# Four column blocks of a branch's output product as two pairs of seven half-size products, in a fused encoder layer

## The reference, cut to what matters

```python
y_a = o_a.reshape(B, S, GLA_HEADS * GLA_DV) @ w_gla_out      # branch A, 1024 x 1024 @ 1024 x 1024
...
y_b = o_b @ w_mla_out                                        # branch B, the same shape
g = jax.nn.sigmoid(gates.astype(jnp.float32)).astype(x.dtype)
merged = g[..., :D] * y_a + g[..., D:] * y_b
return merged @ w_o
```

## Time and profile before

| what | value |
| --- | --- |
| median of 3 runs | 1970.11 us (1969.41 to 1972.61) |
| the profiled execution: time | 1970.56 us |
| its span, first to last instruction | 1968.8 us |
| busy: PE, PEld, DVE, ACT, POOL | 1894.8, 1599.6, 1341.3, 1026.8, 136.4 us |
| mean granted TensorE clock | 0.987 |

### The profile page before, as it was taken

The page is one execution under the profiler, slowest core; times in us unless marked ns, Lnnn a source line. Parts: engine busy times, 40 slices in busy tenths (PEclk is TensorE's granted clock), DMA queues, the critical chain, the costliest instruction groups (busy, mean ns, idle before and its releaser), DMA issues.

```text
span 1968.8 us, 26535 instructions
## 1 busy us (share of the span) xinstructions
PE 1894.8 (96%) x9316; PEld 1599.6 (81%) x9316; DVE 1341.3 (68%) x1802; ACT 1026.8 (52%) x1681; POOL 136.4 (7%) x139
## 2 busy tenths in 40 slices
PE   7999999999999999999999999995699999999998
PEld 7988888888878888888888888885588888888886
DVE  4477777767864656556866334435799898898986
ACT  6465555555563424344534112222377777877775
POOL 1111110111000000000000000000010100101010
PEclk9999999999999999999999999998799999999999
DMA  6100000000311112021353542524899999999993
GB/s 206 43 24 11 23 17 23 17 23 12 118 55 44 55 33 65 21 73 61 124 175 133 173 127 88 191 110 175 314 364 401 394 398 399 389 400 389 398 395 81
DMA packets 146135, 322.04 MB, mean 164 GB/s; under 512 B 17920, under 2 KB 72576, under 8 KB 146048
## 3 DMA queue, kind: packets, MB, share of 16 engines
q1 hardware_dynamic: 141296, 304.09, 41.7%
q0 software_dynamic: 4752, 16.78, 3.4%
HBM read 283.07 MB, written 37.75 MB: 163 GB/s over the span
## 4 chain that ended last, share of the span: by engine, by line
PE 88%; DVE 8%; ACT 2%; issue 1%; DMA 1%; POOL 1%; SPq 0%; ACTq 0%; DVEq 0%; POOLq 0%
PE ps L968 23%; PE ps L970 23%; PE ps L969 23%; PE ps L957 7%; PE ps L1045 5%; PE ps L1254 1%; PE ps L1266 1%; PE ps L1085 1%; PE ps L1084 1%; DVE pT_lo L1521 1%; PE ps L1238 1%; PE ps L1398 1%; PE ps L1264 1%; DVE top_i L2203 1%; DVE qR L1702 1%
## 5 line engine op out<-in xcount | busy, mean ns | idle before, releaser
L1521 DVE TENSOR_TENSOR w_lo<-w_raw,w_hi 128x1024 fp32r<-128x1024 f32 x384 | 442.5, 1218 | 54.9 <-ACT w_hi L2721 54.7
L2721 ACT ACTIVATE w_hi<-w_raw 128x1024 fp32r<-128x1024 f32 x384 | 370.9, 1053 | 11.5 <-DMA w_raw<-in_w_gate_e 11.1
L968 PE MATMUL ps<-w_hi,xeT_hi 128*128 128x512 f32 x512 | 201.2, 393 | 1.8 <-DVE xeT_lo L1521 1.0
L970 PE MATMUL ps<-w_hi,xeT_lo 128*128 128x512 f32 x512 | 199.7, 390 | 0.0
L969 PE MATMUL ps<-w_lo,xeT_hi 128*128 128x512 f32 x512 | 199.2, 389 | 0.0
L1521 DVE TENSOR_TENSOR d_lo<-d_raw,d_hi 128x1024 fp32r<-128x1024 f32 (+1 forms) x64 | 68.1, 1072 | 168.0 <-ACT d_hi L2438 163.4
L1751 DVE TENSOR_REDUCE row_max<-ps 128x1 f32<-128x1024 f32 x64 | 78.3, 1223 | 104.5 <-PE ps L1085 104.4
L2438 ACT ACTIVATE d_hi<-d_raw 128x1024 fp32r<-128x1024 f32 x46 | 48.8, 1061 | 190.3 <-PE ps L970 130.5
L968 PE MATMUL ps<-hT_parts,d_hi 128*128 128x512 f32 x368 | 144.7, 393 | 0.8 <-DVE obS L1774 0.8
L970 PE MATMUL ps<-hT_parts,d_lo 128*128 128x512 f32 x368 | 143.4, 390 | 0.0
L969 PE MATMUL ps<-hT_parts,d_hi 128*128 128x512 f32 x368 | 143.3, 389 | 0.0
(11 more groups left out here) (368 smaller groups left out, 4209.8 us busy)
## 6 DMA issues: line engine op xcount, KB each, us to landing
w_raw<-in_w_gate_e SPq DMA_DIRECT2D x128, 512.0 KB, 7.2
w_raw<-in_w_up_e SPq DMA_DIRECT2D x128, 512.0 KB, 7.0
w_raw<-in_w_down_e SPq DMA_DIRECT2D x128, 512.0 KB, 5.9
d_raw<-in_w_in SPq DMA_DIRECT2D x80, 256.0 KB, 3.2
gates_T<-stage SPq DMA_DIRECT2D x16, 512.0 KB, 2.9
sg<-gates_T SPq DMA_DIRECT2D x16, 512.0 KB, 3.6
xs<-in_x SPq DMA_DIRECT2D x8, 512.0 KB, 12.9
rows_T<-hT SPq DMA_DIRECT2D x2, 2048.0 KB, 6.9
```

The costliest lines, as they stand in the source:

```text
L968: pe.matmul(out_ap, a_hi, b_hi, start=start, stop=False)
L970: return pe.matmul(out_ap, a_lo, b_hi, start=False, stop=stop)
L1521: return dve.tensor_tensor(dst, whole, high.bitcast(F32), ALU.subtract)
L2721: nc.scalar.activation(w_hi[:, n % RING, :], w_raw[:, n % RAW, :], ACT.Copy).then_inc(hi_ok, 1)
```

## The change

The last four blocks of branch B (jobs 12 to 15) become two pairs, numbered p = 6 and 7 behind the six gate pairs. They use the gate stage's scheme with roles changed: the operand is `oT` (branch B's rows), the weight blocks are i = 4, 5 and 6, 7 of `w_mla_out`. The operand sums, four sets of 4 sums with 3 low parts (and a fourth low part later), are made from raw rows that are loaded a second time, under jobs 8 to 11. Gating is done in halves (`y_gate`). Merged rows are all split behind the pairs, since the sums lie where their parts go. The changed lines, cut to those that carry the order:

```diff
@@ SyncE
+            def load_o(k):
+                if k == 0:
+                    sp.wait_ge(oT_lo_ok, 2 * KD)
+                elif k == 1:
+                    sp.wait_ge(d_used, Y0 + KD)
+                else:
+                    sp.wait_ge(o_lo_ok.sem, o_lo_ok.at(3 * (k - 1)))
+                for j in range(2):
+                    sp.dma_start((stage, o_raw_odd)[k % 2][:, j, :], ob_dram[KD // 2 * j + k]).then_inc(o_in[k].sem, 16)
...
-            for m in range(2 * KD):
-                if m + 2 < 2 * KD:
-                    load_job((m + 2) // KD, 1, (m + 2) % KD, Y0 + m + 2)
-                    load_gate(m + 2)
-                if 2 <= m + 2 < KD:
+            for m in range(Y_WHOLE - 2):
+                if m == KD:
+                    load_o(1)
+                load_job((m + 2) // KD, 1, (m + 2) % KD, Y0 + m + 2)
+                if m >= KD - 1 and m != KD + 1:
+                    load_o((0, 2)[m - KD + 1])
+                elif m == KD + 1:
+                    load_o(3)
+                load_gate(m + 2)
+                if m + 2 < KD:
                     load_stage(m + 2)
+            load_pair(PAIRS)
+            load_gate(KD + 4)
+            load_gate(KD + 5)
+            load_pair(PAIRS + 1)
+            load_gate(KD + 6)
+            load_gate(KD + 7)
@@ TensorE, in gate_products
+                    if p == PAIRS:
+                        pe.wait_ge(y_ev, KD + j // 2 + 1)
+                        if j in (2, 3):
+                            pe.wait_ge(o_lo_ok.sem, o_lo_ok.at(12 if j == 2 else 16))
...
-            for m in range(2 * KD):
+            for m in range(Y_WHOLE):
                 branch_job(m)
+            for p in range(PAIRS, PAIRS + Y_PAIRS):
+                gate_products(p)
@@ VectorE
+            def o_sums_of(k):
+                dve.wait_ge(o_in[k].sem, o_in[k].at(32))
+                b11, b12, b21, b22 = o_whole(0, k), o_whole(1, k), o_whole(2, k), o_last(k)
+                dve.tensor_tensor(b11, b12, b11, ALU.subtract).then_inc(o_sum.sem, 1)
+                dve.wait_ge(o_sum.sem, o_sum.at(4 * k + 1))
+                dve.tensor_tensor(b12, b22, b12, ALU.subtract).then_inc(o_sum.sem, 1)
+                dve.tensor_tensor(o_whole(3, k), b22, b11, ALU.subtract).then_inc(o_sum.sem, 1)
+                dve.wait_ge(o_sum.sem, o_sum.at(4 * k + 3))
+                dve.tensor_tensor(b21, b21, o_whole(3, k), ALU.subtract).then_inc(o_sum.sem, 1)
...
+            for k in range(4):
+                if k < 2:
+                    dense_lo(Y0 + KD + k + 2)
+                o_sums_of(k)
+                o_sums_low(k)
+                if k == 2:
+                    weight_sums(p, range(4))
+                elif k == 3:
+                    weights_low(p, (0, 1, 2, 3))
+                    for i in range(4):
+                        o_last_low(i)
+                    weights_low(p, (4,))
+                product(KD + k)
+            weights_low(p, (5, 6))
+            y_sum(p, 0)
+            y_gate(p, 0)
+            weight_sums(p + 1, range(4))
+            weights_low(p + 1, (0, 1))
```

More of the change, by code:

```diff
@@ L55 @@
 Y0 = MERGE0 + len(WHOLE)
-OUT0 = Y0 + 2 * KD
+Y_WHOLE = KD + 4
+Y_PAIRS = 2
+OUT0 = Y0 + Y_WHOLE
 CREDIT = 1
@@ L1347, in _ @@
                 gate_products(p)
-            for m in range(2 * KD):
+            for m in range(Y_WHOLE):
                 branch_job(m)
-            pe.wait_ge(y_ev, 2 * KD - 2)
-            halves_first = [(half, j) for half in range(2) for j in range(4)]
+            for p in range(PAIRS, PAIRS + Y_PAIRS):
+                gate_products(p)
+            free_first = {(0, 0): 1, (0, 2): 2, (0, 3): 4, (1, 2): 4, (1, 3): 4, (1, 1): 5, (0, 1): 6, (1, 0): 7}
             tiles_first = [(half, j) for j in range(4) for half in range(2)]
@@ L1364, in _ @@
                 pe.wait_ge(mT_lo_ok, k + 1)
-                for half, j in halves_first if k == 0 else tiles_first:
-                    if k == 0 and half:
-                        pe.wait_ge(y_ev, 2 * KD - (j < 2))
+                for half, j in free_first if k == 0 else tiles_first:
+                    if k == 0:
+                        pe.wait_ge(p1_ok.sem, p1_ok.at(PAIRS + Y_PAIRS))
+                        pe.wait_ge(u_ok.sem, u_ok.at(SUMS * (PAIRS + Y_PAIRS - 1) + free_first[half, j]))
                     mm = mix_out(j, half, 4 * half + j, k)
@@ L2107, in _ @@
             dense_lo(Y0 + 1)
-            for m in range(2 * KD):
-                if m < KD:
-                    branch_lo(1, m)
+            for m in range(KD):
+                branch_lo(1, m)
                 dense_lo(Y0 + m + 2)
                 product(m)
[L2113 to L2118, removed]
+            p = PAIRS
+            for k in range(4):
[16 more added lines that the diff above has]
+            weights_low(p + 1, (0, 1))
+            y_sum(p, 1)
+            y_sum(p, 2)
+            weights_low(p + 1, (2, 3))
+            y_sum(p, 3)
+            y_gate(p, 1)
+            weights_low(p + 1, (4, 5))
+            y_sum(p, 4)
+            y_sum(p, 5)
+            y_sum(p, 6)
+            y_gate(p, 2)
+            y_gate(p, 3)
+            weights_low(p + 1, (6,))
+            p = PAIRS + 1
+            y_sum(p, 0)
+            y_gate(p, 0)
+            dense_lo(OUT0)
+            y_sum(p, 1)
+            y_sum(p, 2)
+            merged_lo(0)
+            y_sum(p, 3)
+            y_gate(p, 1)
+            merged_lo(1)
+            y_sum(p, 4)
+            y_sum(p, 5)
+            y_sum(p, 6)
+            dense_lo(OUT0 + 1)
+            y_gate(p, 2)
+            y_gate(p, 3)
+            for k in range(2, KD):
+                out_lo(k)
+                merged_lo(k)
             def residual(t, half):
@@ L2673, in _, with o_sums_high, o_last_high @@
             dense_hi(Y0 + 1)
-            for m in range(2 * KD):
-                if m < KD:
-                    branch_hi(1, m)
-                dense_hi(Y0 + m + 2)
[L2678 to L2682, removed]
+            def o_sums_high(k):
+                for n in range(3):
+                    act.wait_ge(o_sum.sem, o_sum.at(4 * k + (1, 2, 4)[n]))
+                    act.wait_ge(d_used, Y0 + KD)
+                    hi, _ = o_split(n, k)
+                    nc.scalar.activation(hi, o_whole(n, k), ACT.Copy).then_inc(o_hi_ok.sem, 1)
+            def o_last_high(k):
+                act.wait_ge(o_sum.sem, o_sum.at(4 * k + 3))
+                act.wait_ge(d_used, OUT0)
+                hi, _ = o_split(3, k)
+                nc.scalar.activation(hi, o_whole(3, k), ACT.Copy).then_inc(o_hi_ok.sem, 1)
+            for m in range(KD):
+                branch_hi(1, m)
+                dense_hi(Y0 + m + 2)
+            for k in range(4):
+                if k < 2:
+                    dense_hi(Y0 + KD + k + 2)
+                o_sums_high(k)
+            weights_high(PAIRS, (0, 1, 2, 3, 4))
+            for k in range(4):
+                o_last_high(k)
+            weights_high(PAIRS, (5, 6))
+            first_product(PAIRS)
+            weights_high(PAIRS + 1, range(PRODUCTS))
+            first_product(PAIRS + 1)
+            act.wait_ge(prod_mm.sem, prod_mm.at(PRODUCTS * (PAIRS + 1) + 2))
+            dense_hi(OUT0)
+            merged_hi(0)
+            merged_hi(1)
+            act.wait_ge(prod_mm.sem, prod_mm.at(PRODUCTS * (PAIRS + Y_PAIRS)))
+            dense_hi(OUT0 + 1)
+            for k in range(2, KD):
+                out_hi(k)
+                merged_hi(k)
             def row_squares(t, half):
```

141 lines of the change are left out of this document (121 added, 20 removed).

## The result

| kernel | median | runs |
| --- | --- | --- |
| before | 1970.66 us | 6 (1968.22 to 1972.61) |
| changed | 1982.84 us | 6 (1981.61 to 1986.35) |

The ratio is 1.0066, with a 95% interval of 1.0057 to 1.0076: slower by 0.7%. (Ratios here are those on record; they can differ a little from the quotient of the two medians, which is 1.0062 here.) The profiled execution took 1982.43 us. The forecast was 1977.8 with a range up to 1982.0, so the sign was right and the size was 5 us short.

What follows compares the result with a forecast made beforehand. TensorE's matmul stream, 0.227 us apart, was taken as the bound. Matmuls saved -5.4, wait ahead of the first pair +11.1, clock and later waits +1.8: +7.5 us, giving a median of 1977.8 us, range 1973.5 to 1982.

Steps and rivals of the forecast that it cites:

- What the change takes from TensorE: In the two new pairs: 24 matmuls fewer at 0.227 us each, 5.4 us less.
- Step 1: Job 10's weights land behind two raw loads at 1173.8; VectorE's sum then releases the SP queue at 1183.1, before 1177.15.
- Step 3: VectorE after job 11's weights: low parts 1189.6, set 1, product, sum 1196.5, SP released 1197.7, set 2 until 1202.1.
- Step 4: First pair's weights, queued behind set 3's raw rows and gate rows, land at 1205.4; alone they would at 1204.0.
- Step 5: VectorE's 10.5 us from those weights to the pair's start, taken as 1215.7; TensorE waits 11.1 us.
- Rival B: Ahead of the first pair: loads in time, only VectorE's work counts; wait 2.8 us, 1969.2 us; chance 0.10.
- rival C: Operand sums run under the jobs, wait under 1.5 us, TensorE's saving shows: 1964.7 to 1966.2 us; chance 0.05.
- step 2: Job 11's weights, behind the late release and set 2's raw rows, land at 1188.5; ScalarE's high parts 5.2 us late.
- clock and these waits are one term, not two: Behind the first pair: time lost to half clock absorbs TensorE's later 1.9 us of waits; together 1.8 us.
- of 3 with the clock loss: Second pair's weights: in by about 1230, ready 1233.7, wanted 1234.7 or later; slack 1 us, 3 with clock loss.
- Rival D: More waits: second pair's cover gone or half clock longer; +11 or more, 1981 to 1984 us; chance 0.15.
- sign of being wrong: First-pair wait under 6 us, loads landing before wanted, or waits over 2 us between pairs or in the mix.

Runs made afterwards that it cites:

- e7: Changed kernel, weights of job 11 and first pair earlier in SP queue, operand sums before low parts, first two output-weight loads before last gate load; 1964.67 us.
- e1: Changed kernel with job 11's weight loads moved up in the SP queue to right behind job 10's; 1974.71 us, 1.0035 of before.
- e3: Changed kernel with both job 11's and the first pair's weight loads moved up in the SP queue; 1971.49 us, 1.0010 of before.
- e4: Changed kernel, same queue, operand-sum sets 0 and 1 ahead of the weights of jobs 10 and 11 on VectorE and ScalarE; 1970.66 us.
- e6: Changed kernel with 115 unused identity transposes put into TensorE's wait ahead of the pairs; 1981.42 us, 1.0065 of before.
- e2: Changed kernel with only the first pair's weight loads moved up, ahead of set 3's raw rows and job 11's gate rows; 1977.04 us.

## Why the prediction was right in kind and short in size

**Right, step by step.** *What the change takes from TensorE*: 5.4 us; e7 measured 5.46. *Step 1*, from the gate load ahead of job 10's weights to their high parts: 1173.8 - 1165.96 = 7.8 us, measured 1174.14 - 1166.14 = 8.0; from there to the release 9.3, measured 9.2. *Step 3*, from landing to sum: 8.0 us, measured 1198.25 - 1190.30 = 7.95. *Step 4*, from the release to the pair's weights: 7.7 us, measured 7.9. *Step 5*, from there to TensorE's start: its terms add up to 10.5 us, and the 1215.7 that was taken leaves 10.3; measured 1217.64 - 1207.38 = 10.26. So VectorE's durations, bounded by 0.61 and 0.72 us from the weight sums, held. e1 to e3 show that the two releases of the SP queue are the cause: without them 10.2 of the 13.5 us are gone. e4 shows what makes the releases late, the order of VectorE's work. Rival B's sum (2.8 us) has 3.3 us of e3 beside it, and rival C's saving turned up whole in e7.

**Mis-sized: step 2, the weights of job 11.** The prediction issued them at 1183.5 and 1184.0 and let the last land at 1188.5, 4.5 us on. Measured, the last was issued at 1184.2 and landed 6.1 us later, at 1190.3:

```profile
L693 SPq DMA_DIRECT2D d_raw<-in_w_mla_out x2: 434/470/507, 1183.7 to 1184.2; - x2
...
DMA to landing us min/median/max: 4.6/5.3/6.1
```

The raw rows ahead of them were 0.5 us late (issued at 1181.3, landed 4.6 later, at 1186.0; forecast 1185.5). Behind these, the gate rows and the weights took 4.3 us for 1 MB, where I had put 1.4 + 1.6. I had added up single distances from the earlier trace rows, a place where the weights have one load of 512 KB ahead of them. The trace of before has six places with two such loads ahead, the weights of jobs 3 to 8, with gate rows and staged rows. Two of them:

```profile
L643 SPq DMA_DIRECT2D d_raw<-in_w_gla_out x2: 432/470/507, 1115.4 to 1115.9; - x2
...
DMA to landing us min/median/max: 5.1/5.3/5.5
...
L643 SPq DMA_DIRECT2D d_raw<-in_w_gla_out x2: 432/470/507, 1125.7 to 1126.2; - x2
...
DMA to landing us min/median/max: 5.1/6.0/6.8
```

Five of the six have their last landing 5.4 to 5.7 us after issue, one 6.8. With those, step 2 would have ended at 1189.4 to 1190.8, and it ended at 1190.3.

**Left out: what happens ahead of step 1.** The two profiles have different axes: job 8 starts at 1161.27 before and at 1160.59 after. Counted from there, forecast and measured are these:

| event | forecast | measured | late by |
| --- | --- | --- | --- |
| gate load ahead of job 10's weights | 4.7 | 5.55 | 0.9 |
| high parts of job 10 | 12.5 | 13.55 | 1.0 |
| release of the SP queue | 21.8 | 22.75 | 0.9 |
| weights of job 11 | 27.2 | 29.7 | 2.5 |
| weights of the first pair | 44.1 | 46.8 | 2.7 |
| first pair starts | 54.4 | 57.05 | 2.6 |
| fourth job ends | 43.3 | 43.5 | 0.2 |

So step 2 added 1.6 us, and 0.9 were there before step 1 began: the forecast took the place of that gate load from the profile before, as if nothing moved ahead of it. In the changed kernel it waits for job 9's weights and the work behind them, and their last landing took 5.6 us, against 4.3 before. What is new there is two loads of raw rows issued right behind them (1157.60). That these are the reason is not shown: in the seven experiments, which have the same loads there, the gate load goes 4.3 to 5.2 us after job 8's start. With 0.1 from the later steps and less the 0.2 of the fourth job's end, that is the wait's 2.4 us beyond the forecast, and 13.5 lies beyond the 9.2 to 13.0 that I had allowed.

**Failed: "clock and these waits are one term, not two".** In kind it holds: the mix begins when VectorE is through, and in e6 nothing of the gain on the clock reached it (argued from one profile each). But the term rests on the length of the chain from the first pair's start to the mix. That was put at 38.6 us (1215.7 to 1254.3), and it was 41.1 (1217.64 to 1258.75), while TensorE was through after 39.67. Two landings are in it. The second pair's weights were put 14.3 us behind the pair's start and were in after 15.4, at 1233.04, again with a last load of 6.1 us:

```profile
L813 SPq DMA_DIRECT2D d_raw<-in_w_mla_out x4: 383/507/508, 1225.4 to 1227.0; - x4
...
DMA to landing us min/median/max: 3.8/4.8/6.1
```

The other is the first output weights. From the sum of block 5 to their landing the prediction had 4.7 us (1244.6 to 1249.3). Measured:

```profile
1246.69 1.22 DVE L2179 TENSOR_TENSOR carry<-carry,sg 128x1024 f32<-128x1024 f32 x1
...
1253.80 1.06 ACT L2625 ACTIVATE d_hi<-d_raw 128x1024 fp32r<-128x1024 f32 x1 [6.43 <-DMA d_raw<-in_w_o]
```

That is 7.1 us from the sum's start, or 6.0 from its end; 5.4 of them lie between the issue of these weights (1248.39), right behind a gate load, and their high part. The prediction doesn't say whether its 1244.6 is the start or the end of the sum, so the output weights make up between 1.3 and 2.4 of the 2.5 us, and the second pair's landing, at most 1.1, the rest.

The cover "of 3 with the clock loss" held for the pair itself, which didn't wait. Behind it TensorE waited 1.43 + 0.92 = 2.35 us in the mix on top of the 1.6 us that it had lost to the clock (put at 1.8, measured 1.6). A further 0.5 us of longer steps behind the waits stood in no term. So the forecast's +7.5 lacks 2.4 of the wait and 2.9 behind the pairs, less 0.2 of clock: 5.1 us, the distance to +12.6.

**The cause in one line.** The landings of loads were put too early, by 1.6 us at job 11's weights, by some 0.9 ahead of job 10's, and by up to 2.5 us behind the first pair, and passed undiminished through a chain without slack. My bounds for them, "0.2 us and 5%", came from the same quiet place as their sizes. Rival D, "more waits", +11 or more, had a chance of 0.15 and described the outcome; the pair's cover itself held, what broke was the mix behind it. The sign of being wrong, waits over 2 us in the mix, came as two waits of 2.35 us together, neither of them over 2.

**Not settled.** How much of the 6.1 us is the loads ahead and how much a packet of the instruction queue, which no run here turns on or off (last section).

## What to carry to other kernels

In a queue that issues in order, a load stands behind every wait ahead of it: list for each new load the waits in front of it, and who releases them. Here three places of that kind, and the order of work on the engine that releases them, hid a saving of 5.5 us and cost 12 more, and moving five calls in the queue's program and in those of VectorE and ScalarE (no instruction more or less) gave all of it back; that was found only by undoing them one after another, since each repair showed the next wait. When a releaser is an engine that works in order too, order its work by what is already there (raw rows) ahead of what is still coming (weights). And take a landing's size and its range from places of the trace where as much stands ahead of it, not from one where it is alone.

## What the runs showed that was not expected

**Late last landings.** Both loads of 6.1 us, and the one of 6.8 us in the kernel before, coincide with a packet of the queue that the DMA view lists as "q8 instruction", among the packets of the 16 DMA engines. The view of the changed kernel, from the issue of job 11's weights to their landing (queue, kind: packets, MB, share):

```profile
q8 instruction: 1, 0.02, 1.0%
```

1.0% of 16 engines over 6.4 us is 1 us on one engine. In all nine profiles the load of job 6's weights has such a packet 4 to 5 us after its first issue, and a last landing of 6.7 to 6.9 us, where that of job 5's, of the same make-up, has none and 5.2 to 5.5. Both kernels have 56 such packets in all. But a packet in the window is neither enough nor needed. In the kernel before, the weights of jobs 3 and 14 have one near the end of the load and land after 5.6 and 4.3 us, like their neighbours without; in e6 one ran from 1231.0, again near the end, and the last load took 5.1 us. And in the changed kernel the weights of job 10, with three loads of 512 KB issued within 1.3 us ahead of them and no such packet, have a last landing of 6.2 us. Shown is a coincidence that repeats at one place in nine profiles, not a cause, and beside it a landing just as late with more loads ahead and no packet; how the two share the 6.1 us is open.

**The clock behind waits of different length.** Waits of TensorE ahead of the pairs, and what the granted clock did:

| kernel | wait us | clock |
| --- | --- | --- |
| e4 | 1.3 | stays 1.00 |
| e3 | 3.3 | 0.50 from 0.4 before its end, 3.0 us behind it |
| e1 | 6.1 | 0.50 from 2.8 before its end, 4.1 us behind it |
| e2 | 10.3 | 0.50 for most of it, 3.1 us behind it |
| changed | 13.5 | 0.50 for most of it, 3.1 us behind it |

A half-speed stretch of 3.0 to 4.1 us costs 1.5 to 2 us, and the waits of 3.3 and of 13.5 us paid about the same.
